# Attention branch of a hybrid decoder layer: seven block products, rows merged by transfers

## The reference

```python
proj = h @ w_in                      # q, k, v, cb, cc, cu, ga, gb
a = sliding_window_attention(rope(q), rope(k), v, sinks)   # 1024 wide, blocks of 128 tokens
b_out = cb * causal_dwconv(cc * cu)                        # 1024 wide
branch_a = a @ w_attn_branch         # 1024 -> 2048
branch_b = b_out @ w_conv_branch     # 1024 -> 2048
merged = sigmoid(ga + b_gate[0]) * branch_a + sigmoid(gb + b_gate[1]) * branch_b
x = x + rmsnorm(merged @ w_o, g_mix_post)
```

## Time and profile before

| what | value |
|---|---|
| median of the runs | 2649.99 us (3 runs, 2649.57 to 2650.19) |
| profiled execution: span from first to last instruction | 2648.5 us |
| median less span | 1.5 us |
| mean granted TensorE clock | 1.000 |
| conv branch, first matmul of line 1306 to first of line 1328 | 738.1 to 820.0 us |
| attention branch, to the first matmul of w_o | 820.0 to 911.8 us |
| HBM read, written | 420.63 MB, 55.71 MB |

### The profile page before, as it was taken

One profiled execution on the slowest core, in us unless ns is written; L12 is line 12 of the kernel. 1 busy time (PEld: TensorE's weight loads), 2 busy tenths in 40 slices (PEclk: granted clock), 3 DMA queues, 4 the chain that ended last, 5 costly groups with the idle time before them and its releaser, 6 DMA issues.

```text
span 2648.5 us, 55450 instructions
## 1 busy us (share of the span) xinstructions
PE 2641.1 (100%) x20949; PEld 2582.9 (98%) x20949; DVE 2221.4 (84%) x3913; ACT 1386.6 (52%) x2533; POOL 189.5 (7%) x289
## 2 busy tenths in 40 slices
PE   9999999999999999999999999999999999999999
PEld 8999999999999999999999999999999999999899
DVE  7988888888896687898888888888888768789987
ACT  6544555555563255655555555555555453445454
POOL 0221000000010000000000000000000000000000
PEclk9999999999999999999999999999999999999999
DMA  6676334333484355655566555665569575565774
GB/s 229 187 209 184 134 117 142 133 124 117 158 262 160 131 165 158 247 174 161 169 206 186 181 162 167 191 198 175 158 188 306 158 239 173 162 207 162 251 265 151
DMA packets 160028, 479.65 MB, mean 181 GB/s; under 512 B 17177, under 2 KB 51361, under 8 KB 156480
## 3 DMA queue, kind: packets, MB, share of 16 engines
q1 hardware_dynamic: 128752, 370.81, 39.7%
q0 software_dynamic: 30960, 106.59, 18.0%
q10 hardware_dynamic: 144, 0.15, 0.0%
HBM read 420.63 MB, written 55.71 MB: 180 GB/s over the span
## 4 chain that ended last, share of the span: by engine, by line
PE 97%; DVE 2%; issue 0%; ACT 0%; DMA 0%; SPq 0%; DVEq 0%; ACTq 0%
PE pair L1208 78%; PE pair L1173 6%; PE pair L1328 3%; PE pair L1306 3%; PE pair L1111 2%; PE pair L935 1%; PE pair L1285 1%; PE pair L1133 1%; PE pair L987 1%; PE pair L1008 1%; DVE v_lo L1977 0%; DVE lo L2328 0%; PE pair L997 0%; DMA s_raw<-in_sstream 0%; PE pair L1068 0%
## 5 line engine op out<-in xcount | busy, mean ns | idle before, releaser
L1208 PE MATMUL pair<-o_hi,v_hi 128*128 128x260 f32 x5840 | 1657.6, 284 | 1.2 <-DVE v_lo L1977 0.8
L1208 PE MATMUL pair<-o_hi,v_lo 128*128 128x260 f32 x5840 | 1650.1, 283 | 0.0
L1404 ACT ACTIVATE v_hi<-s_raw 128x512 fp32r<-128x512 f32 (+1 forms) x1368 | 852.1, 626 | 931.3 <-PE pair L1208 795.3
L1208 PE MATMUL pair<-lo,v_hi 128*128 128x260 f32 x4172 | 1179.3, 283 | 0.0
L1977 DVE TENSOR_TENSOR v_lo<-s_raw,v_hi 128x512 fp32r<-128x512 f32 (+1 forms) x1288 | 874.0, 681 | 301.1 <-ACT v_hi L1404 265.1
L1208 PEld LDWEIGHTS pair<-o_hi,v_hi 128*128 128x128 f32 x5840 | 1099.0, 188 | 14.9 <-issue 11.9
L1208 PEld LDWEIGHTS pair<-o_hi,v_lo 128*128 128x128 f32 x5840 | 1100.8, 188 | 0.0
L1208 PEld LDWEIGHTS pair<-lo,v_hi 128*128 128x128 f32 x4172 | 784.8, 188 | 0.2
L1208 PE MATMUL pair<-lo_E,v_hi 128*128 128x260 f32 x834 | 236.2, 283 | 0.0
L1404 ACT ACTIVATE v_hi<-s_one 128x512 fp32r<-128x512 f32 (+1 forms) x220 | 137.1, 626 | 189.1 <-PE pair L1208 164.5
L1208 PE MATMUL pair<-lo_A,v_hi 128*128 128x260 f32 x834 | 235.3, 282 | 0.0
(11 more groups left out here) (287 smaller groups left out, 2494.7 us busy)
## 6 DMA issues: line engine op xcount, KB each, us to landing
s_raw<-in_sstream SPq DMA_DIRECT2D x468, 512.0 KB, 4.9
s_one<-in_sstream POOLq DMA_DIRECT2D x168, 512.0 KB, 5.4
raw<-f_scr SPq DMA_DIRECT2D x12, 1040.0 KB, 7.6
s_raw<-in_sstream SPq DMA_DIRECT2D x32, 384.0 KB, 4.0
g_scr<-d_h SPq DMA_DIRECT2D x16, 520.0 KB, 2.7
g_in<-g_scr SPq DMA_DIRECT2D x32, 260.0 KB, 2.8
x_scr<-y_sb SPq DMA_DIRECT2D x8, 1040.0 KB, 5.3
s_one<-in_sstream POOLq DMA_DIRECT2D x16, 384.0 KB, 4.8
```

Source lines behind the costliest of these rows:

```text
L1208: mm = pe.matmul(out, wt[:, slot, kk * P:kk * P + P], r[:, k, :], start=j in (0, 1, 3) and k == 0 and n == 0, stop=k == nk - 1 and n == 2, ...
L1404: nc.scalar.activation(v_hi[:, n % 4, 0:width], src, ACT.Copy, scale=0.5 if halved(u) else 1.0).then_inc(v_hi_rdy, 1)
```

## The change

Stages: the attention branch becomes units `U_AT` = 40 to 47 of the same kind as the conv units (`branch_unit` on every engine), and w_o begins at unit 48. The attention steps are reordered (`step_of`), so that a group of two rows is complete after each fourth step; DVE then makes its forms (`attention_form`, four operations of 260 columns) and POOL stores all seven forms to `af_scr` with two transfers. SP loads the forms (`af_load`), ACT and DVE split them (`af_high`, `af_low`: 1040 columns each), five in conv units 35 to 39, two at the turn to unit 40. The attention result goes to a ring of four buffers `acc`; DVE gates it there, and POOL adds it to the conv row by an accumulating transfer (`merge`), all but the last two rows, which DVE adds. The gates of conv rows 4 to 15 move out of the conv units: attention units 41 to 46 gate four rows each, at slots 1, 3, 5 and 6. `add_conv_sum` is cut into `first_half` and `second_half`, with `merge` between them, and the first sum of w_o's unit 48 comes by transfer too. `t1` of w_o is placed in units 44 and 46, `s3`, `t2(1, 0)`, `t3(1, 0)` in unit 47.

```diff
-U_O = U_BR + KD // 2
+U_AT = U_BR + KD // 2
+U_O = U_AT + KD // 2
+def step_of(n):
+    return n % 4, n // 4
+def gates_of(u):
+    i = u - U_AT
+    if u <= U_BR:
+        return []
+    if u < U_BR + 3:
+        return [2 * (u - U_BR) - 2, 2 * (u - U_BR) - 1]
+    if i < 1:
+        return []
+    attention = [KD + 2 * i - 2, KD + 2 * i - 1]
+    return attention + ([2 * i + 2, 2 * i + 3] if i < KD // 2 - 1 else [])
...
+        def rows_merged(eng, rows):
+            eng.wait_ge(merged_in, 32 * min((rows + 1) // 2, KD // 2 - 1))
+            if rows > KD - 2:
+                eng.wait_ge(merged_ready, rows - KD + 2)
...
             for u in range(U_BR, U_O):
+                if u == U_BR + 2:
+                    sp.wait_ge(af_stored, 32 * 4)
+                    af_load(0, 1, 2, 3, 4)
+                if u == U_AT - 1:
+                    for j in range(2):
+                        product_done(u, j)
+                        af_load(5 + j)
                 if u % 2:
                     load(r_of(u) + 2)
+                for m in gates_of(u):
+                    next_gate(GATE_AT[m])
...
+            def branch_unit(u):
+                hi, lo = (cf_hi, cf_lo) if u < U_AT else (af_hi, af_lo)
                 for j in range(7):
                     banks_free(None, u, j, u % 2)
+                    if u in (U_BR, U_AT):
+                        pe.wait_ge(br_rdy, j + (1 if u == U_BR else 8))
                     pe.wait_ge(v_lo_rdy, n + 1)
                     for k in range(KC):
-                        for i, (wt, r) in enumerate(((v_hi, cf_hi[j]), (v_hi, cf_lo[j]), (v_lo, cf_hi[j]))):
+                        for i, (wt, r) in enumerate(((v_hi, hi[j]), (v_hi, lo[j]), (v_lo, hi[j]))):
-            def branch_step(m, p):
...
-            with pe.Fori(1, KD // 2) as i:
-                for p in range(2):
-                    branch_step(2 * i + p, p)
...
-                    act.wait_ge(v_used, BR_H + (0 if j < 5 else 2 * KD))
+                    act.wait_ge(v_used, BR_H)
+                        if u >= U_AT + 4:
+                            act.wait_ge(merged_in, 32 * (u - U_AT - 3))
+                        copied(u, 0, d11, r1_out)
...
+                    if U_BR + 3 <= u < U_AT and j == 2:
+                        af_high(u - U_BR - 3)
+                    if u == U_AT - 1 and j == 6:
+                        af_high(5)
+                    if u == U_AT and j == 0:
+                        af_high(6)
...
+                if u in TURN and TURN[u] % 4 == 3 and i in (11, 12, 13):
+                    attention_form(TURN[u] // 4, {11: 1, 12: 2, 13: 4}[i])
...
+            def attention_gated(m):
+                row = acc[u % 4][:, m % 2, :]
+                dve.scalar_tensor_tensor(out=row, in0=g_in[p % 4][:, :], scalar=1.0, in1=row,
+                                         op0=ALU.add, op1=ALU.mult).then_inc(br_free, 1)
+            def add_last(m):
+                dve.wait_ge(br_free, GATE_AT[KD + m] + 1)
+                dve.tensor_tensor(x_tile(m), x_tile(m), two(acc[(U_O - 1) % 4][:, m % 2, :]), ALU.add)\
+                   .then_inc(merged_ready, 1)
...
+                gate_slots = (1, 3, 5, 6) if u > U_AT else (1, 6)
+                gates = dict(zip(gate_slots, gates_of(u)))
...
-                    if U_BR + 1 < u < U_O - 2 and j in (3, 5):
-                        br_low(rows_split(u) + j // 5)
+                    if u == U_BR + 1 and j in (3, 4, 5, 6):
+                        attention_form(3, {3: 1, 4: 2, 5: 4, 6: 6}[j])
+                    if U_BR + 3 <= u < U_AT and j == 6:
+                        af_low(u - U_BR - 3)
+                    if u == U_AT and j in (2, 3):
+                        af_low(3 + j)
+                    if u == U_AT + 4 and j == 6:
+                        rows_merged(dve, 4)
+                        t1(1, 0)
+                    if u == U_AT + 6 and j == 6:
+                        rows_merged(dve, KH)
+                        t1(1, 1)
+                    if u == U_O - 1 and j == 2:
+                        both_halves(s3, U_O)
+                    if u == U_O - 1 and j == 5:
+                        rows_merged(dve, KH + 4)
+                        t2(1, 0)
+                    if u == U_O - 1 and j == 6:
+                        t3(1, 0)
-            def branch(m):
...
+            for m in (KD - 2, KD - 1):
+                attention_gated(m)
+                add_last(m)
+            rows_merged(dve, KD)
...
+            def merge(u):
+                i = u - U_AT
+                if i:
+                    pool.wait_ge(merged_in, 32 * i)
+                for n in range(2):
+                    pool.wait_ge(br_free, GATE_AT[KD + 2 * i + n] + 1)
+                    pool.dma_start(x_tile(2 * i + n), two(acc[u % 4][:, n, :]), accum_op=ALU.add)\
+                        .then_inc(merged_in, 16)
+            first_half(U_BR + 4)
+            for u in range(U_BR + 2, U_O - 2):
+                second_half(u + 2)
+                if u > U_AT:
+                    merge(u - 1)
+                if u + 3 < U_O:
+                    first_half(u + 3)
+            merge(U_O - 3)
+            first_half(U_O)
+            second_half(U_O)
+            merge(U_O - 2)
```

More of the change, by code:

```diff
@@ L223, in build @@
         pT_sb = sub("pT_sb", [P, 2, 4, BLK])
-        a_st = [sub(f"a_st{i}", [P, 2, BLK]) for i in range(2)]
+        aw = sub("aw", [P, 2, T])
         assert o[0] <= r_g + KD * XB
@@ L360, in by_dma @@
             return (2 <= u < U_CONV + 6 or u == U_SIG + 1 or U_BR <= u < U_O
-                    or u > U_O and u not in PLAIN)
+                    or u >= U_O and u not in PLAIN)
         def sums_of(u, h):
@@ L552, in build @@
         a_rdy = sem("a_rdy")
-        a_stored = [sem(f"a_stored{i}") for i in range(2)]
-        br_in = [sem(f"br_in{i}") for i in range(4)]
+        af_rdy = sem("af_rdy")
+        af_stored = sem("af_stored")
+        merged_in = sem("merged_in")
         br_hi_rdy = sem("br_hi_rdy")
@@ L683, in h_store, with af_load @@
                 sp.dma_start(dram, d_h[u % 2][:, :, :]).then_inc(h_stored[u % 2], 16)
[L685 to L689, removed]
+            def af_load(*forms):
+                for j in forms:
+                    sp.dma_start(af_raw[j][:, :, :], af_scr[CONV_FORM_AT[j], :, :, :]).then_inc(op_in[j], 16)
             def cf_load(*forms):
@@ L1769, in conv_unit @@
                         sigmoid_g(U_BR - 1, j - 3)
-                    if U_BR + 1 < u < U_O - 2 and j in (2, 4):
-                        br_high(rows_split(u) + j // 4)
-            for u in range(U_BR, U_O):
-                conv_unit(u)
-            for m in range(KD - 2):
-                v_high(BR_S + 2 * m + 4)
-                v_high(BR_S + 2 * m + 5)
-                if m == 2:
-                    warm(ACT.Sqrt, 2)
+                    if U_BR + 3 <= u < U_AT and j == 2:
[4 more added lines that the diff above has]
+                        af_high(6)
+                    if u == U_AT and j == 2:
+                        warm(ACT.Sqrt, 2)
+            for u in range(U_BR, U_O):
+                branch_unit(u)
             by(1, wo_evac)
@@ L2744, in conv_unit @@
                         sums(u, 7, d11, d12, d22)
-                    if u > U_BR and j in (1, 6):
-                        conv_gated(m - 2 + j // 6)
+                    if j in gates:
+                        branch_gated(gates[j])
                     if u == U_BR and j == 2:
```

296 lines of the change are left out of this document (140 added, 156 removed).

## The result

Before 2650.19 us (2649.57 to 2650.29, 5 runs), after 2660.83 us (2658.60 to 2663.92, 5 runs): ratio 1.0041, 95% interval 1.0028 to 1.0053. The change is slower by 10.6 us, where 2643.0 was forecast with a range of 2639.5 to 2648.5. The profiled execution has a span of 2658.4 us for 2648.5 before, 9.9 more.

What follows compares the result with a forecast made beforehand. PE was taken as the bound, busy for the whole span. Terms -11.5 - 0.6 + 1.1 + 1.9 + 1.1 + 0.8 = -7.2 us took the span from 2648.5 to 2641.3; runs lie 1.5 above, so 2643, range 2639.5 to 2648.5.

Steps and rivals of the forecast that it cites:

- Fewer matmuls: Attention stage: 672 matmuls in place of 768, 96 fewer at 0.1195 us each, -11.5 us.
- Four gates in a unit: Units 41 to 47: DVE's work fits, but product 6 starts 0.16 us late in each of seven units, +1.1 us.
- the conv units' gaps: Four conv units no longer pay 0.16 us at product 6, -0.6 us; the first conv unit's three gaps stay.
- The turn to unit 40: Two wide af_low splits on DVE delay products 5 and 6 of unit 40, +1.9 us, bounds 0 and 2.3.
- t1 in units 44 and 46: 1.15 us more DVE work in slot 6 delays the next product 6, two times 0.55, +1.1 us, bounds 0 and 2.3.
- The turn to w_o: w_o's start: DVE's later s2 delays product 2, the last accumulating transfers may add, +0.8 us, bounds 0 and 4.
- Rows by transfers: Attention forms stored and loaded for conv units 35 on arrive in time, 0 us, bounds 0 and 2.
- The weight sums become the bound: Rival, chance 0.08: merges lengthen POOL's weight-sum rounds to 12.5 us for a 10.2 unit, +12, 2655 us.
- Late transfers: Rival, chance 0.26: forms, gates or last merged rows late at several places, +2 to +6 on the forecast, 2645 to 2649.
- the port trap: Merges in POOL's queue: DVE might shut POOL out while it writes descriptors; doubted, an accumulating issue took 0.86 beside busy DVE.

Runs made afterwards that it cites:

- e1: The changed kernel with the 14 accumulating transfers to conv rows left out, waits moved to the gate; 2645.42 us.
- e5: The changed kernel with the weight sums of even and odd branch units on two semaphores, merges kept; 2656.15 us.
- e13: The changed kernel with two semaphores and weight sums' first reads (units 36 to 47) in SP's queue, unit 36's ahead of the attention form loads; 2655.72 us.
- e4: Against the changed kernel: no merges by transfer, DVE adds the rows, conv rows gated in the conv units again; 2646.84 us.
- e3: The changed kernel with the first read of the next weight sum ahead of the merges in POOL's queue; 2658.31 us.
- e8: The changed kernel with each merge a plain copy of the row instead of an accumulating one; 2650.54 us.
- e7: The changed kernel with each merge moving only the first half of its row (260 of 520 columns); 2649.85 us.
- e2: The changed kernel without the second, adding read of each weight sum from unit 36 to w_o's first, merges kept; 2649.53 us.
- e6: Against the changed kernel: DVE adds the rows, conv rows gated in conv units, two semaphores, pieces moved at the turns to unit 40 and w_o; 2645.07 us.

## Why the prediction was wrong

The step that failed is the additions of merged rows, which "leave DVE for POOL's queue" at no price in the sum: they cost 15.4 us (e1). They did it by making gates, weight sums and the last merged rows late. The prediction knew these paths but priced each too low and apart: sums in one rival (0.08), gates in another (+2 to +6), the last rows in the turn to w_o (up to 4). Point by point:

- *Fewer matmuls, -11.5.* Right: a unit that waits for nothing takes 10.07 us, 0.1199 a matmul where 0.1195 was taken. Without merges (e1) the two branch stages take 904.83 - 737.96 = 166.9 us. The 166.5 of the prediction is a slip of its own: it takes all of the 7.2 off the stages, though 0.8 of it was to fall behind the start of w_o. By its own sum they should take 165.7, and e1 is 1.2 above.
- *Four gates in a unit; the conv units' gaps.* Right: 0.17 in units 41 to 43, DVE busy 61.3 of 64 in e1; the conv stage is 0.4 (e1) to 0.7 shorter, for 0.6.
- *The turn to unit 40, +1.9.* Right: products 5 and 6 start 0.80 + 0.86 = 1.7 over the step of 0.12, and unit 40 is 1.9 longer than a unit without waits.
- *t1 in units 44 and 46, +1.1.* In e1, product 6 of units 45 and 47 is 0.8 late each, where the prediction put it, with 0.3 in unit 46. By the units' lengths (10.95, 10.46 and 10.95 for 10.23) it is 1.7: the right mechanism, 0.6 too small.
- *The turn to w_o, +0.8 for DVE's order and the last transfers.* In e1, without merges, 0.2 is lost at product 2 and 0.9 at product 6, 1.0 by the end: right in size by luck, since most of it lies at a product that was not looked at. In the changed kernel the last transfers cost 4.2 at product 1, which waits for s_one and which this step did not look at, and 2.5 at product 2: 7.5 in all behind the start of w_o. The upper bound of 4 was too low.
- *Rows by transfers, 0.* Right for the forms: no wait of PE in units 35 and 36. The merges were not in this step's sum at all, and they are the 15.4.
- *The weight sums become the bound, 0.08.* This rival came nearest in time, in part by luck. Sums were late in the changed kernel, which is 5.8 above its 2655. But e5 and e13 took the late sums away and kept 10.7 and 10.3 of the 15.4, by late gates and at the turn to w_o. Its rounds were put at 12.5 and took 15.0. Merges landed in 7.0, not in the 5.0 taken from the earlier trace rows; an issue took 1.36, not the 0.86 of the earlier trace rows; first reads landed in 5.6 (3.1 to 8.9), not in the 4.8 of the earlier trace rows. "Merges fall into a wait of 5.0 that exists anyway" looked at POOL's time alone; it did not ask what else the DMA engines had to carry.
- *Late transfers, 0.26.* Gates and the last merged rows did come late, by up to 2.0 and 6.0 in the changed kernel, so this mechanism is true beside the sums. Its bound of +6 was too low: with the sums in time it came to 10.7 over e1 (e5). "Most have a unit's time in hand" did not hold for the gates, of which four are loaded in a unit through a ring of four buffers.

Without merges the forecast's mechanism stands, some 2 us short: e1's median is 2645.4 for 2643 forecast, its profiled span (of one of the faster runs) 2642.6 for 2641.3. With them, 15.4 us come back. The trap was to price a transfer by its queue (issue time, order, a landing of the nearest row). The earlier trace rows held the warning: a conv unit, with the same sums and gates, keeps the DMA engines busy for 0.71, next to 0.45 in the attention tiles. The change made the attention tiles into eight such units, moved two conv gates more into six of them, and put 14 new transfers of a row on top.

The prediction's doubt about the port trap held: a pair of plain merges, with the source in SBUF, was issued in 1.74 us beside DVE busy for 59.5 of 64, 0.87 each, as a second read (0.86). The 2.7 of an accumulating pair goes with the kind of transfer, not with DVE.

Shown by runs: that merges are the cost (e1); that it is not DVE's load (e1, e4); that the order in POOL's queue is worth 2.5 (e3) and the wait of a read behind the sum before 4.7 at most (e5); that taking the first reads out of POOL's queue gives nothing more (e13 against e5); that late sums are not needed for most of it (e5, e13); that plain merges in place of accumulating ones take away two thirds (e8), and halving them as much (e7), so that these shares do not add up; and that merges slow transfers of SP's queue (the gates' landing). Argued only: that it is the busy share of the DMA engines by which they do it. The shares of 0.81 without merges, 0.90 with plain ones and 0.96 with accumulating ones go with 2645, 2650 and 2661, and e7 has 0.93 and 2650; but e2 has 0.98 and 2649.5. There the second reads are gone, and the share alone does not tell the time: it depends on what waits.

## What to carry to other kernels

Before work of a busy engine is handed to transfers, read the DMA engines' share of the stage that takes it, not only the queue, and ask for every transfer of that stage, in whatever queue, how much later it may land. Here a stage at 0.81 hardly waited (e1), at 0.96 it did; where between them it turns was not measured. Price an accumulating transfer apart from a plain one. An engine that looks full may still be the better place: 14 more additions of 0.6 us on DVE (e4, e6) cost less than the transfers that were to spare them.

## What the runs showed of the hardware

- An accumulating transfer of 128 x 520 fp32 within SBUF took 1.36 us to issue in a pair and 7.0 (4.5 to 13.9) to land, in 256 packets of 1040 bytes, 27.0 us of engine time; a plain one took 0.9 and 5.3 (2.5 to 9.4), in 64 packets of 4160 bytes, 11.9 us. Together with the reads beside it the first moved 250 GB/s at a busy share of 0.96, the second 290 at 0.90.
- The granted clock fell to half after PE's longest wait in the attention stage, 2.8 us at 873.91: from the full 2.4 GHz to 1.2. Two of the starts that followed, and the window behind the wait (columns as above):

```profile
874.29 0.42 PE L1317 MATMUL pair<-af_lo,v_hi 128*128 128x260 f32 x1
874.50 0.42 PE L1317 MATMUL pair<-af_hi,v_lo 128*128 128x260 f32 x1
```

```profile
873.90:877.20 3.30, 3.29 (x15) 3.30 (x16) 1.80 (x4) 1.55 (x4) 1.59 (x2) 0.50 1.09 202
```

  Steps are 0.21 instead of 0.12, for some 15 matmuls, about 1.4 us. The last column but one, the busy share, is above 1 here, so it is not exact over a stretch this short. Product 1 of w_o, behind its wait of 4.05, took 5.29 in place of 3.67 (this cost nothing more, since product 2 waited for the last merges anyway). So a long wait can cost more than its length. Its length does not tell by itself: the clock fell behind waits of 2.3 in e2 and e7, and stayed full behind 2.24 at 899.09 and behind 2.88 at the turn to w_o in e8. The waits of 0.6 in e1 left the window's clock at 1.00.
